# The expert V product with the gated activations stationary and 512 columns of V moving, the residual turned onto the sums by TensorE, and the next norm with tokens on partitions

## The reference

```python
def peer_ffn(x, wq, keys, u, v):            # PEER_EXPERTS = 128 * 128, 8 heads, top 16
    ...
    gate = jax.nn.softmax(best_s, axis=-1)
    ue = u[idx]
    ve = v[idx]
    act = jax.nn.gelu(jnp.einsum('td,thkd->thk', xc, ue).astype(jnp.float32), approximate=False)
    return jnp.einsum('thk,thkd->td', (gate * act).astype(xc.dtype), ve)

def layer_norm(x, g, b):
    mu = jnp.mean(xf, axis=-1, keepdims=True)
    var = jnp.mean(jnp.square(xf - mu), axis=-1, keepdims=True)
    return ((xf - mu) * lax.rsqrt(var + LN_EPS) * g + b).astype(x.dtype)

for l in range(DEPTH):
    ...
    h = layer_norm(DN_ALPHA * h + mix, ln1_g[l], ln1_b[l])
    ffn = peer_ffn(h, peer_wq[l], peer_keys[l], peer_u[l], peer_v[l])
    h = layer_norm(DN_ALPHA * h + ffn, ln2_g[l], ln2_b[l])
```

## Time and profile before

| | value |
|---|---|
| median of three runs | 3517.38 us |
| the profiled execution | 3517.11 us |
| its span (first to last instruction) | 3515.3 us |
| PE busy | 3163.8 us (90%), 21028 matmuls |
| PEld busy (weight loads, beside PE) | 2851.3 us (81%) |
| DVE busy | 2293.4 us (65%) |
| ACT busy | 1380.3 us (39%) |
| POOL busy | 232.2 us (7%) |
| HBM read | 437.34 MB, 125 GB/s over the span |

### The profile page before, as it was taken

One profiled execution on the slowest core, in us unless ns is written; L12 is line 12 of the kernel. 1 busy time (PEld: TensorE's weight loads), 2 busy tenths in 40 slices (PEclk: granted clock), 3 DMA queues, 4 the chain that ended last, 5 costly groups with the idle time before them and its releaser, 6 DMA issues.

```text
span 3515.3 us, 61175 instructions
## 1 busy us (share of the span) xinstructions
PE 3163.8 (90%) x21028; PEld 2851.3 (81%) x21028; DVE 2293.4 (65%) x4989; ACT 1380.3 (39%) x2330; POOL 232.2 (7%) x405
## 2 busy tenths in 40 slices
PE   4999998977888997967999999989889689999997
PEld 2888887766676777857999999867778589999997
DVE  3677666246765654997666666665569966666665
ACT  2222222234652442144444444334321444444442
POOL 0000000000000000083000000000001910000000
PEclk7999999998999998999999999999999999999998
DMA  5232331222122233402555555422324035555552
GB/s 220 107 119 95 117 122 67 84 88 97 59 77 79 96 116 100 155 24 84 180 184 185 179 180 190 155 84 96 120 96 144 0 122 186 181 179 183 186 182 83
DMA packets 71711, 439.64 MB, mean 125 GB/s; under 512 B 7168, under 2 KB 8576, under 8 KB 27456
## 3 DMA queue, kind: packets, MB, share of 16 engines
q1 hardware_dynamic: 69088, 420.33, 33.9%
q0 software_dynamic: 2384, 17.11, 1.4%
q10 hardware_dynamic: 144, 0.98, 0.1%
HBM read 437.34 MB, written 1.05 MB: 125 GB/s over the span
## 4 chain that ended last, share of the span: by engine, by line
PE 80%; DVE 11%; ACT 4%; DVEq 2%; issue 2%; DMA 1%; ACTq 0%; SPq 0%
PE bank L449 20%; PE bank L450 19%; PE bank L451 19%; PE bank L1931 6%; PE bank L1296 3%; PE bank L1949 2%; DVE arena L2132 1%; ACT arena L2028 1%; PE bank L1096 1%; PE bank L798 1%; PE bank L1222 1%; DVE arena L1311 1%; PE bank L787 1%; PE bank L1218 1%; PE bank L533 1%
## 5 line engine op out<-in xcount | busy, mean ns | idle before, releaser
L433 DVE TENSOR_TENSOR peer_r<-wring,peer_r 128x512 fp32r<-128x512 f32 x1264 | 838.9, 688 | 478.5 <-ACT peer_r L428 477.0
L428 ACT ACTIVATE peer_r<-wring 128x512 fp32r<-128x512 f32 x1264 | 783.9, 629 | 761.4 <-PE bank L451 751.4
L449 PE MATMUL bank<-peer_r 128*128 128x256 f32 x2048 | 579.6, 283 | 0.0
L450 PE MATMUL bank<-peer_r 128*128 128x256 f32 x2048 | 579.6, 283 | 0.0
L451 PE MATMUL bank<-peer_r 128*128 128x256 f32 x2048 | 579.6, 283 | 0.0
L449 PE MATMUL bank<-res_r,peer_r 128*128 128x256 f32 x1664 | 475.9, 286 | 36.9 <-DVE peer_r L433 36.6
L450 PE MATMUL bank<-res_r,peer_r 128*128 128x256 f32 x1664 | 474.7, 285 | 0.0
L451 PE MATMUL bank<-res_r,peer_r 128*128 128x256 f32 x1664 | 474.6, 285 | 0.0
L449 PE MATMUL bank<-h_r,peer_r 128*128 128x512 f32 (+1 forms) x1088 | 395.8, 364 | 46.8 <-DVE peer_r L433 30.8
L449 PEld LDWEIGHTS bank<-peer_r 128*128 128x128 f32 x2048 | 393.2, 192 | 0.0
L450 PEld LDWEIGHTS bank<-peer_r 128*128 128x128 f32 x2048 | 393.2, 192 | 0.0
(11 more groups left out here) (340 smaller groups left out, 4436.3 us busy)
## 6 DMA issues: line engine op xcount, KB each, us to landing
wring<-in_w_peer SPq DMA_DIRECT2D x256, 1024.0 KB, 4.8
wring<-in_w_proj SPq DMA_DIRECT2D x34, 1024.0 KB, 4.8
wring<-in_w_hy SPq DMA_DIRECT2D x32, 1024.0 KB, 5.3
arena<-in_w_ada POOLq DMA_DIRECT2D x16, 1024.0 KB, 5.1
wring<-in_w_out SPq DMA_DIRECT2D x16, 1024.0 KB, 4.8
wring<-in_w_ada SPq DMA_DIRECT2D x8, 1024.0 KB, 8.8
wring<-in_w_hyout SPq DMA_DIRECT2D x8, 1024.0 KB, 4.9
wring<-in_w_q SPq DMA_DIRECT2D x8, 1024.0 KB, 4.8
```

The lines of the kernel that those rows point to most:

```text
L428: act.activation(SPLIT[:, buf, 0, :], raw_quarter(name, i, j, q), ACT.Copy).then_inc(split_hi, 1)
L433: v.tensor_tensor(SPLIT[:, buf, 1, :], raw_quarter(name, i, j, q), SPLIT[:, buf, 0, :].bitcast(F32), ALU.subtract).then_inc(split_lo, 1)
L449: pe.matmul(out_ap, w_hi, x_hi, start=start, stop=False, **kw)
L450: pe.matmul(out_ap, w_hi, x_lo, start=False, stop=False, **kw)
```

## The change

The V unit is turned round: 128 tokens of gated scores are stationary, and the 512 columns of the unit's V are moving. A unit is then 6 matmuls of 512 columns (two groups of 128 tokens, three terms) in place of 12 of 256. The sums have tokens on partitions: bank 4 + 2 tt + half holds 128 tokens (group tt) by 512 features. Units 0 and 1 (U) stay as they were.

The banks are no longer zeroed. PE multiplies the high and low part of h by an identity (`IDW`, 384 columns, the identity in the middle and zeros on both sides), which writes the residual, turned so that tokens are on partitions, onto the sums before the first V product: 32 matmuls with 256 moving columns. DVE writes IDW earlier, with a memset and a copy behind the gates' normalisation. The factor ALPHA is taken out of the residual: the gates are divided by it, and the norm's eps becomes 1e-5 / ALPHA^2 (`epsh`).

The norm has tokens on partitions. DVE takes mean and variance of each half bank with `bn_stats` and `bn_aggr`, the halves of a unit apart, the first of them while the last V unit runs. ACT and DVE scale and shift the sums into `XN`, PE transposes it back in 16 transposes into banks 0 to 3, and ACT and DVE apply the norm's g and b on the way to h. ACT runs a one-column square root ahead of the `post` phase. The semaphores of the first block's heads are merged without a change of order.

```diff
-            v.tensor_tensor(g0, g0, wide(MXS[:, 1, :], 2, TOPK), ALU.mult)
+            v.scalar_tensor_tensor(g0, g0, 1.0 / ALPHA, wide(MXS[:, 1, :], 2, TOPK), ALU.mult, ALU.mult)
+            v.memset(IDW[:, :].bitcast(F32), 0.0)
+            v.drain()
+            v.tensor_copy(IDW[:, P:2 * P], ident).then_inc(wide_ident, 1)
             v.drain().then_inc(ijg_ready, 1)
...
-            v.drain()
-            v.wait_ge(g_in, GROUPS * (l + 1) + 4)
-            for b in range(4, 8):
-                a = v.memset(bank[b][:, :], 0.0)
-            a.then_inc(acc_zero, 1)
+            v.drain().then_inc(gated_done, 1)
...
+            pe.wait_ge(wide_ident, l + 1)
+            pe.wait_ge(gated_done, l + 1)
+            pe.wait_ge(g_in, GROUPS * (l + 1) + 4)
+            for tt in range(2):
+                for k in range(KT):
+                    turn = IDW[:, P:3 * P] if k % 2 == 0 else IDW[:, 0:2 * P]
+                    acc = token_bank(tt, k // 4)[:, (k % 4) // 2 * T:((k % 4) // 2 + 1) * T]
+                    pe.matmul(acc, h_hi[:, k, tt * P:(tt + 1) * P], turn, start=(k % 4 == 0), stop=False)
+                    pe.matmul(acc, h_lo2[:, k, tt * P:(tt + 1) * P], turn, start=False, stop=(k % 4 == 3))
...
+            def rows_product(half, buf, par):
+                v_hi, v_lo = SPLIT[:, buf, 0, :], SPLIT[:, buf, 1, :]
+                for tt in range(2):
+                    s = slice(tt * P, (tt + 1) * P)
+                    mm = mm3(pe, token_bank(tt, half)[:, :], GPR[:, par, 0, s], GPR[:, par, 1, s], v_hi, v_lo,
+                             False, True, skip_group_check=True)
+                mm.then_inc(unit_used, 1)
...
+        def tokens_tensor(pe, l):
+            for k in range(KT):
+                if k % 4 == 0:
+                    pe.wait_ge(tok_act, 2 * l + k // 4 + 1)
+                    pe.wait_ge(tok_dve, 2 * l + k // 4 + 1)
+                for tt in range(2):
+                    mm = pe.transpose(bank[k // 2][:, (k % 2) * T + tt * P:(k % 2) * T + (tt + 1) * P],
+                                      XN[:, tt, k * P:(k + 1) * P], ident)
+                if k % 2:
+                    mm.then_inc(tok_turned, 1)
+            pe.wait_ge(h_tok, 4 * (l + 1))
+
+        def tokens_scalar(act, l, g, b):
+            act.wait_ge(tok_var, l + 1)
+            act.activation(TSD, TMV[:, :, 1], ACT.Sqrt, scale=1.0, bias=C["epsh"]).then_inc(tok_sd, 1)
+            act.wait_ge(tok_mean, l + 1)
+            for half in range(2):
+                act.activation(XN[:, 0, half * 512:(half + 1) * 512], token_bank(0, half)[:, :], ACT.Identity,
+                               scale=TSD[:, 0:1], bias=TNM[:, 0:1]).then_inc(tok_act, 1)
+            for k2 in (1, 3):
+                act.wait_ge(tok_turned, 4 * l + k2 + 1)
+                for k in (2 * k2, 2 * k2 + 1):
+                    a = act.activation(h[:, k, :], bank[k2][:, (k % 2) * T:(k % 2 + 1) * T], ACT.Identity,
+                                       scale=g[:, k:k + 1], bias=b[:, k:k + 1])
+                a.then_inc(h_tok, 1)
+
+        def tokens_vector(v, l, name, n, g, b):
+            for half in range(2):
+                v.wait_ge(unit_used, unit_of(name, 0, n - 2 + half) + 1 + UNITS)
+                for tt in range(2):
+                    v.bn_stats(TST[:, tt, half, :], token_bank(tt, half)[:, :])
+            v.drain()
+            for tt in range(2):
+                v.bn_aggr(TMV[:, tt, :], TST[:, tt])
+            v.drain().then_inc(tok_var, 1)
+            v.wait_ge(tok_sd, l + 1)
+            v.reciprocal(TSD, TSD)
...
```

More of the change, by code:

```diff
@@ L255, in program @@
         GA = Carve(BLOCKS * T + c5.at).take(T)
+        IDW = arena_r("ident_r", BLOCKS * T + 2 * UNITS * UNIT, 3 * P)
         c5 = Carve(BLOCKS * T)
@@ L1013, in prep_tensor @@
             for g in range(KV_HEADS):
-                pe.wait_ge(ksq, g + 1)
-                pe.matmul(bank[2 + g][:, :], ones, PRB[:, g, :], start=True, stop=True).then_inc(kss, 1)
+                pe.wait_ge(head_sq, g + 1)
+                pe.matmul(bank[2 + g][:, :], ones, PRB[:, g, :], start=True, stop=True).then_inc(head_ss, 1)
             for g in range(KV_HEADS):
@@ L1983, in peer_tensor @@
                     pe.wait_ge(split_lo, unit_of(name, i, UNITS * j + q) + 1)
-                    for m in range(4):
-                        w, d = slice(m * P, (m + 1) * P), m0 + m
-                        mm = mm3(pe, bank[4 + d // 2][:, (d % 2) * T:(d % 2 + 1) * T], SPLIT[:, q, 0, w],
-                                 SPLIT[:, q, 1, w], GPR[:, par, 0, :], GPR[:, par, 1, :], False, True,
-                                 skip_group_check=True)
-                    mm.then_inc(unit_used, 1)
+                    rows_product(q % 2, q, par)
         def peer_scalar(act, l):
```

129 lines of the change are left out of this document (69 added, 60 removed).

## The result

Four runs of the changed kernel took 3435.91 to 3439.22 us, with a median of 3436.89 us. Four runs of the kernel before on the same chip gave 3516.95 us. The ratio is 0.9774, with a 95% interval of 0.9757 to 0.9791, so the kernel is 80.1 us faster. The forecast was 3432 us with a range of 3424 to 3448.

What follows compares the result with a forecast made beforehand. PE was taken to bound the loop, with standstills at layer ends and loop entry. Terms -40.3 (V units), -44.6 (ends), -1 (first product), 0 (entry), +1 (IDW) sum to -84.9 us: 3432 us, range 3424 to 3448.

Steps and rivals of the forecast that it cites:

- Loop: V units of both layers' loops: 6 matmuls of 512 columns for 12 of 256, 1.440 to 1.362 us each, -40.3 us.
- The rule of N/2.4 + 2.5 ns: Skill's matmul gap for V units, set against the forecast's price: the edit would bring 8 us, not 40; total 3464 us.
- Layer ends: Last V matmul to store or next layer's first product: 30.0 and 29.4 us to 7.4 each, -44.6 us together.
- The doubt about the clock: Layer end's 16 transposes may run at either clock: 2.3 us at full, about 4.0 at half, 3.0 taken.
- First product: Next layer's first product, 16 matmuls behind the layer end: -1 us taken, bounds 0 and -2.3.
- Entry: Start of each loop, memsets replaced by 32 residual matmuls: 0 for both layers, bounds -2.5 and +8 us.
- done by about 1622: Sign of being right at the loop's entry: the 32 residual matmuls finished by about 1622 us.
- IDW: Memset and copy behind the gates' last DVE line delay PE: +0.5 us per layer, +1 in all, bounds 0 and 1.4.
- The stream isn't paid by the column: Rival on V units: 512 columns cost 0.240 us, so they bring nothing; total 3472.5 us, chance 5%.
- the ends are 8.0 and 7.2 us: Rival on layer ends: 12 us each from two-pass statistics, low clock and slow hand-overs; total 3441 us, chance 16%.
- the entry lost 0.55 us in one layer: Rival on the loop's entry: all 56 matmuls at low clock in both layers, +8 us, 3440 us, chance 7%.
- the V matmul kept its rate: Rival on V matmuls: they leave the fp32r rate, for example 0.454 us each, some 4130 us, slower than before; chance 2%.

Runs made afterwards that it cites:

- the repetition: The changed kernel run and profiled again without an edit, against the kernel before: 3436.29 us, ratio 0.9770.
- after: The changed kernel as first profiled, against the kernel before: profiled execution 3439.22 us, median of its four runs 3436.89 us.

## Why the prediction was right, and where it was off

**Loop.** The steps of the prediction, 0.120 us for a matmul of 256 columns, 0.227 for one of 512, and PE as the bound throughout, were right. The loops give 18.55 and 18.53 us, where 20.15 each were forecast, and undoing the width alone gives exactly these back. The term was mis-sized by 3.2 us of 40.3. The unit takes 2.75 / 2 = 1.375 us inside a block and not 1.362, since the first five matmuls behind the U units are up to 0.01 us slower; the row of the first block that I took the price from the earlier trace rows is a stream of 512 columns with no U units between. That alone would be 5 us over the 384 units in blocks; the U units, 0.01 us shorter per block, gave 1.5 back, and the 128 units of the `post` phases took 1.36 us, as forecast. The 37.1 us also lie below the 39 from which the range was built, a bound that the prediction gave no reason for. The reasoning behind the price, a fixed part per matmul, holds between 256 and 512 columns and fails at 128. The rule of N/2.4 + 2.5 ns that the prediction sets against it is called the gap of an isolated matmul in that section of the Trainium skill, which has other figures for a stream of weight loads and matmuls; its 216 ns lie below the 227 of this trace.

**Layer ends.** 44.6 us forecast, 21.37 + 22.89 = 44.3 measured. The steps hold singly. The late statistics end 1.33 us behind V end (1.4 forecast) at 0.690 us per pass, the price of the reduction in the earlier trace rows. The small instructions take 1.22 us (1.2), the first half of XN 1.0 (0.8), the transposes 3.35 and 2.52 us (3.0 for each), the last evictions with their hand-over 1.1 (1.0). The doubt about the clock was in place: one end has the transposes mostly at the low clock, the other half and half, and with the clock held up they take 1.94 us. No table load stands between the last V unit and the square root; it lies ahead of the `post` phase, as forecast. The prediction's upper bound of 10.5 us for an end doesn't follow from its steps, which give 7.4 + 2.8 + 1.0 = 11.2; nothing came near it.

**First product.** 5.80 us went to 3.56 us, start to next product, so -2.2 where I took -1 within bounds of 0 and -2.3. That is one execution. In the repetition the same product took 5.30 us, and in the profiled executions of the other kernels with the changed layer end it is either 3.56 or between 5.29 and 5.75. All four kernels with idle matmuls in the layer end have 3.56. So that PE had just made the transposes doesn't settle the clock there; the -2.2 was luck within the bounds.

**Entry.** I took 0 between -2.5 and +8. In the first layer it is +0.55 us (9.72 to 10.27 us from DVE's last line to the third unit), in the second about -1.5. (Before took 9.72 us in the first layer and 10.21 in the second, both mostly at the low clock.) The difference is the clock. The first layer's windows:

```profile
1618.10:1621.60 3.50, 3.40 (x16) 3.43 (x17) 1.29 (x2) 0.46 (x1) 0.00 (x0) 0.52 0.00 0
1621.60:1623.60 2.00, 2.00 (x18) 2.00 (x18) 0.00 (x0) 0.00 (x0) 0.00 (x0) 0.99 0.00 0
```

The first 16 of 56 matmuls are at the low clock and the rest at the full one; in the second layer the residual ran at 0.12 us from the start. The 16 slow ones cost 16 x (0.214 - 0.120) = 1.5 us, and without them the first layer's entry would be 8.8 us, as the second's is. My mark "done by about 1622" was missed at 1623.6 for that reason, and since PE started 0.6 us later than I took it.

**IDW.** +0.3 us per layer, +0.5 forecast. The 0.6 us in the expectation for the repetition counts in another 0.3 us, by which after is already late at the first layer's first product, 1085.00 against 1084.75 us.

**What was missing.** The sum was -84.9, the profiled executions give -77.95 up to the store, and the medians -80.1. Terms of the forecast explain 3.2 (loop) and 0.3 (ends) of the difference of 7 us, while first product and entry came out some 2 us better than costed and IDW 0.3. The step that failed is one that the prediction didn't have. It took every stretch without an edit as unchanged, and the second layer's stretch from the end of the first product to the G stage is some 5.5 us longer in the profiled execution (5.8 less the 0.3 of `IDW`). The windows tie this to the granted clock, and filling PE's pause in one place of it made it shorter. That the total landed 5 us from the forecast owes something to luck, since these errors go both ways.

How much of the 5.5 us the change itself causes stays open. In the first layer the stretch is the same in both kernels, 411.00 and 411.34 us. In the second it wanders: 406.56 us in the one kept execution of before, and 407.90, 407.97, 408.90, 409.67, 411.41, 411.46, 412.20 and 412.37 in the eight of changed kernels without idle matmuls in the mixer, 407.90 among them with V at 256 columns. Where the first product is slow the stretch is often short, so it is fairer to take both together: 412.4 us in before and 412.5 to 416.8 in the eight. So the change doesn't always bring the low clock, but none of the eight was below before, and what decides where the clock falls was not found. The Trainium skill, page "TensorE: Matmul & The Clock Gate", section "What's actually happening", calls the number of slow matmuls variable from run to run of one kernel; this trace agrees, with 6.46 and 5.41 us for the same 16 matmuls in two executions.

None of the rivals came true. The stream isn't paid by the column (its case was 3472.5 us, which is about the 3475 us of the kernel with 256 columns, where V gains nothing); the ends are 8.0 and 7.2 us (7.6 and 8.0 in the repetition) and not 12; the entry lost 0.55 us in one layer and not 8 in two; the V matmul kept its rate.

## What to carry to other kernels

Where PE is the bound and every matmul has its own weight load, count matmuls as well as columns, find the width below which narrower matmuls no longer get cheaper, and take the distance of starts from a row of the same width and type, inside the same mixture of widths if there is one. A new chain of small steps at the end of a stage can be priced to within a few per cent from neighbouring rows, one by one; its uncertain part is the clock of the matmuls at its end. And a forecast of 0.1% on a kernel with pauses of PE has to leave some microseconds for stretches that no edit touches: if the time matters, try to fill such a pause with idle matmuls that end before the work is there; seven that outlasted it gained nothing here, three that fitted made the stretch behind them 3.4 us or more shorter in the first layer of both kernels that have them.

## What the runs showed of the hardware

- fp32r matmuls with their own weight load, at the full clock: 0.227 us apart at 512 columns, 0.120 at 256 and 0.111 at 128. Halving 512 is nearly linear, halving 256 brings next to nothing.
- Behind a stream of 256 columns the first matmuls of 512 stand 0.23 to 0.24 us apart for about five matmuls (1.17 us in the block shown), the next seven 0.226. Why is not shown.
- The statistics instruction takes 0.690 us for 512 elements out of PSUM, as much as a reduction of the same size, and two aggregations 0.28 us.
- 16 fp32 transposes of 128 x 128 take 1.94 us behind a busy PE, and behind 3.56 us of standstill 2.52 to 3.40 us in the four ends of after and its repetition. In the end shown the granted clock is 1.00 over the standstill and 0.55 over the transposes.
- The same eight fp32 matmuls of 256 columns (16 rows) behind a pause of PE of 3.3 us or a little more took from 3.72 to 6.49 us in different layers and executions, and 3.62 or 3.72 in all with idle matmuls in that pause.
- A plain fp32 matmul of 512 columns is two rows of 0.43 us, nearly four times the 0.227 us of one in fp32r.
